# Where VectorE puts three weight splits among the forms of x, at the front of the last two feed-forwards

## The reference, cut to what matters

```
x = layer_norm(ALPHA * x + mix, ln1_g, ln1_b)
u = depthwise_conv_centred(x @ w_up, conv_w, conv_b)        # w_up: 1024 x 5632, 3 taps along the tokens
gate, val = split(u, 2)                                     # 22 tiles of 128 channels each
ffn = (silu(gate) * val) @ w_down                           # w_down: 2816 x 1024
x = layer_norm(ALPHA * x + ffn, ln2_g, ln2_b)
```

## Time and profile before

| | |
|---|---|
| median of 3 runs | 3225.05 us (3224.18 to 3225.34) |
| time of the profiled execution | 3225.85 us |
| span of the profiled execution | 3224.0 us |
| mean granted clock of TensorE | 0.995 |
| busy, share of the span | PE 98%, PEld 81%, DVE 58%, ACT 44%, POOL 42% |
| DMA | 288.40 MB, mean 89 GB/s |

### The profile page before, as it was taken

The page is one execution under the profiler, slowest core; times in us unless marked ns, Lnnn a source line. Parts: engine busy times, 40 slices in busy tenths (PEclk is TensorE's granted clock), DMA queues, the critical chain, the costliest instruction groups (busy, mean ns, idle before and its releaser), DMA issues.

```text
span 3224.0 us, 43797 instructions
## 1 busy us (share of the span) xinstructions
PE 3163.0 (98%) x17576; PEld 2597.2 (81%) x17576; DVE 1862.2 (58%) x2975; ACT 1419.4 (44%) x2559; POOL 1370.2 (42%) x788
## 2 busy tenths in 40 slices
PE   7999999999999999999999999999999999989998
PEld 4876888888875557888886888899997788879997
DVE  5877366323337663423325686388872768468885
ACT  4323422222246774423334545355553544455554
POOL 2221423232254445444552234645555234445555
PEclk9999999999999999999999999999999999999999
DMA  7323334122132002333232120422233121213231
GB/s 270 110 97 119 127 101 153 54 63 69 51 116 103 14 14 92 113 89 110 74 124 79 46 67 20 142 79 98 97 120 112 46 67 49 63 58 107 97 99 67
DMA packets 88246, 288.40 MB, mean 89 GB/s; under 512 B 10059, under 2 KB 12683, under 8 KB 87276
## 3 DMA queue, kind: packets, MB, share of 16 engines
q1 hardware_dynamic: 88044, 285.60, 27.2%
HBM read 283.47 MB, written 2.10 MB: 89 GB/s over the span
## 4 chain that ended last, share of the span: by engine, by line
PE 87%; DVE 3%; issue 3%; POOL 3%; ACT 2%; DMA 1%; SPq 0%; POOLq 0%; DVEq 0%; ACTq 0%
PE ps L611 16%; PE ps L614 15%; PE ps L612 15%; PE ps L3429 4%; PE ps L3428 4%; PE ps L3427 4%; PE ps L670 2%; PE ps L672 2%; PE ps L671 2%; PE ps L2262 2%; PE ps L3114 1%; PE ps L590 1%; PE ps L585 1%; POOL WL L559 1%; PE ps L586 1%
## 5 line engine op out<-in xcount | busy, mean ns | idle before, releaser
L559 POOL TENSOR_TENSOR WL<-ring,WH 128x1024 fp32r<-128x1024 f32 (+4 forms) x461 | 961.6, 2091 | 1340.9 <-ACT WH L549 1340.5
L549 ACT CAST WH<-ring 128x1024 fp32r<-128x1024 f32 (+4 forms) x497 | 448.9, 904 | 507.4 <-PE ps L614 385.8
L611 PE MATMUL ps<-FR,WH 128*128 128x512 f32 x1120 | 419.2, 374 | 0.2
L611 PE MATMUL ps<-HX,WH 128*128 128x512 f32 x1048 | 413.8, 395 | 4.2 <-DVE WL L537 4.2
L614 PE MATMUL ps<-HX,WL 128*128 128x512 f32 x1048 | 411.9, 393 | 0.0
L612 PE MATMUL ps<-HX,WH 128*128 128x512 f32 x1048 | 410.5, 392 | 0.0
L612 PE MATMUL ps<-FR,WH 128*128 128x512 f32 x1120 | 410.0, 373 | 0.0
L614 PE MATMUL ps<-FR,WL 128*128 128x512 f32 x1120 | 389.2, 373 | 0.0
L611 PEld LDWEIGHTS ps<-FR,WH 128*128 128x128 f32 x1120 | 210.4, 188 | 45.6 <-DVE FR L3327 1.1
L612 PEld LDWEIGHTS ps<-FR,WH 128*128 128x128 f32 x1120 | 210.5, 188 | 36.0
L611 PEld LDWEIGHTS ps<-HX,WH 128*128 128x128 f32 x1048 | 197.6, 189 | 48.6 <-DVE WL L537 4.7
(11 more groups left out here) (456 smaller groups left out, 7049.6 us busy)
## 6 DMA issues: line engine op xcount, KB each, us to landing
ring<-in_ffn_w_up SPq DMA_DIRECT2D x88, 512.0 KB, 3.6
ring<-in_w_up SPq DMA_DIRECT2D x88, 512.0 KB, 3.6
ring<-in_w_mod SPq DMA_DIRECT2D x64, 512.0 KB, 3.8
ring<-in_w_in_tok SPq DMA_DIRECT2D x40, 512.0 KB, 3.7
ring<-in_w_mod_columns SPq DMA_DIRECT2D x32, 512.0 KB, 4.3
ring<-in_w_in_feat SPq DMA_DIRECT2D x32, 512.0 KB, 3.5
ring<-in_w_down SPq DMA_DIRECT2D x48, 320.0 KB, 3.9
ring<-in_ffn_w_down SPq DMA_DIRECT2D x32, 384.0 KB, 3.1
```

The lines of the kernel that those rows point to most:

```text
L549: act.copy(WH[:, p % SPLITS, 0:n], src).then_inc(*split.a.up("high", p))
L559: pool.tensor_tensor(WL[:, p % SPLITS, 0:n], unit_source(p)[0], WH[:, p % SPLITS, 0:n], ALU.subtract).then_inc(*low_up(split.g, p))
L611: pe.matmul(o, high, xh, first, False)
```

## The change

The third unit's split goes from POOL to DVE, in layer 1 alone. `forms_v` gets another order in both layers, and the two splits of `between` are taken apart: `between(0)` is that of the fourth unit, `between(1)` that of the fifth.

```
-        in_vector |= {g_.last for t_ in L_ffb for g_ in (*t_.groups[3:5], *t_.groups[-8:])}
+        in_vector |= {g_.last for t_ in L_ffb for g_ in (*t_.groups[3:5], *t_.groups[-8:])}
+        in_vector.add(L_ffb[1].groups[2].last)
...
-            for k in range(4):
+            def form(k):
                 (wait for the kept tile k + 4, and the three instructions of form k)
-            for k in range(4):
-                if k == 2:
-                    between()
-                low(k)
+            form(0)
+            form(1)
+            low(0)
+            between(0)
+            low(1)
+            form(2)
+            form(3)
+            low(2)
+            between(1)
+            low(3)
...
+            if L.groups[2].last in in_vector:
+                rest_v(dve, L.groups[2].last)
             sums_1_2(FRONT)
-            forms_v(dve, qf, lambda: (rest_v(dve, L.groups[3].last), rest_v(dve, L.groups[4].last)))
+            forms_v(dve, qf, lambda x: rest_v(dve, L.groups[3 + x].last))
             sums_1_2(FRONT + 1)
```

## The result

The changed kernel takes 3231.53 us (median of 16 runs, 3229.79 to 3234.39), the kernel before 3226.11 us (16 runs, 3224.18 to 3228.22): 5.4 us more, ratio 1.0017 with the interval 1.0011 to 1.0024. Forecast were 3226.5 us and a range up to 3229.6: it is slower than that. The new waits came as forecast; the clock behind them, and what PE waits further on, did not. The forecast started from 3225.05 us, the median of three runs; with 16 runs the kernel before lies 1.1 us higher. As a difference the range ended at +4.55 us, and +5.4 was measured. It is 0.17%, less than the 0.2% that I had taken for the least that can be told, and with 16 runs of each kernel it is clear of the noise.

A forecast was written before the change was run, and what follows sets the result against it. PE, busy 98% of the span, was taken to bound the kernel, so only its waits count. +2.5 us in layer 0 and -1.1 in layer 1 gave +1.4 on 3225.05, so 3226.5 us; range 3223.8 to 3229.6.

The forecast's parts named there:

- Fourth unit in layer 1: Layer 1: PE's wait for the fourth unit shrinks from 4.25 to 2.0 us, the unit beginning 3.6 us earlier.
- the fifth: Layer 1: PE waits 2.0 us for the fifth unit, beginning it 4.5 us ahead of before.
- the sixth: Layer 1: PE waits about 3.2 us for POOL's split of the sixth unit; 1.1 us of lead are left.
- Layer 0: DVE's later taps delay POOL's split of the sixth unit; PE newly waits 2.3 to 2.7 us, 2.5 taken.
- The low part of 2.22 us: Layer 1: DVE's low part of x, slowed during POOL's split, returns to 0.74 us; PE is 1.3 us earlier.
- the sum of +1.4: Whole kernel: +2.5 us in layer 0 less 1.1 in layer 1; the forecast itself, chance 0.62.
- the price of the clock: Behind the new waits in both layers: a clock fall costs 0 to 2.9 us each; nothing was taken.
- the idle stretch that kept it: 2844 to 2849 us: PE idle 2.0 of 5 us with the clock at 1.00; reason for pricing falls at nothing.
- Behind it PE takes the sixth unit and the seventh and goes on: Layer 1, behind the sixth unit's wait: PE goes on; a gain of 0.7 to 1.5 us is kept.
- That adds 0 to 0.4: Layer 0, tenth unit: DVE's late fourth sum may delay ACT's cast and POOL's split, adding 0 to 0.4 us.
- The fourth rival: The clock falls in both layers, at PE's restart at the sixth unit: +7.2 us, 3232.3 us; chance 0.04.
- The warning that I had cited: Gaps without matmuls halve PE's rate; by it each longer wait would cost 2.9 us, giving the second or fourth rival's time.

The follow-up runs named there:

- e4: The changed kernel with idle matmuls filling PE's new waits (11 in layer 0; 8, 8, 13 in layer 1); +4.3 us against the kernel before (1.0013).
- e6: The changed kernel run once more, unaltered; 3230.46 against 3225.11 us for the kernel before, +5.35 (1.0016).
- e8: The changed kernel with the third unit's split of layer 1 back on POOL; 3232.18 against 3225.11 us for the kernel before, +7.1 (1.0022).
- e2: The kernel before with the new order in layer 0 alone, layer 1 as before; 3228.20 us, +2.6 against the kernel before (1.0011).
- e12: The kernel before run once more for a second profile of its one long wait; 3225.38 against 3225.39 us, 0.0.
- e1: The changed kernel with layer 0's old order back, layer 1 as changed; 3227.55 against 3225.56 us for the kernel before, +2.0 (1.0005).
- e3: The changed kernel with ACT casting the sixth unit early, ahead of the first gate's silu; 3233.28 against 3225.56 us for the kernel before, +7.7 (1.0025).
- e11: e1 with idle matmuls filling layer 1's three waits (8, 8, 13); +1.5 us against the kernel before (1.0002).
- e7: The kernel before with 18 idle matmuls in PE's one long wait, ahead of layer 1's fourth unit; -1.0 us against the kernel before (0.9997).
- e9: e5 with DVE doing the low part of the first tile's result sooner; 3223.14 against 3225.39 us for the kernel before, -2.3 (0.9992).
- e5: The kernel before with layer 1 reordered on DVE and ACT after what the waits need; 3226.37 against 3225.11 us, +1.3 (1.0002).

## Why the prediction was wrong

**The waits were right.** Fourth unit in layer 1: forecast 2.0, measured 1.9; the fifth (seen in e4, where filling keeps the clock: 7.47 us from the fourth to the fifth, less 5.44) 2.0 and 2.0; the sixth 3.2 and 3.0. Layer 0: forecast 2.3 to 2.7, measured 2.5; at full clock the stretch up to the seventh unit costs 2.8 us (e6), against the 2.5 taken. Layer 1 up to the seventh unit without a fall is 41.98 us, 0.86 less than the profile before; forecast 1.1. DVE stood 1.1 us ahead of the fourth unit's split in layer 0, as said. The low part of 2.22 us went, for 1.15 us of gain (e8), against the 1.3 that I took. Up to the seventh unit, then, the sum of +1.4 is measured as +1.9.

**The first step that failed is the price of the clock**: "A fall costs at most the 2.9 us seen, at least nothing; I take nothing, since three of the four are nearer to the idle stretch that kept it". The runs say otherwise. The duration of the unit behind each wait, at full clock 5.6 us with its start:

| wait of PE | kernel: duration of the unit behind it, us |
|---|---|
| 4.25 | before 8.32, e2 7.16, e12 7.10 |
| 3.0 | after 8.28, e1 7.17, e6 7.19, e8 5.57 |
| 2.48 | after 7.16, e8 7.22, e2 5.57, e6 5.57 |
| 1.94 | clock 0.77 in after, e1, e6 and e8, and in e3 behind 1.90 (hidden) |
| filled | e4 5.58 and 5.57, e11 5.58, e7 5.61 |

The clock fell behind half of the waits of 2.5 us, behind three of four of 3.0, and behind all four of 1.94. Three kernels with another order add four waits: it fell behind 1.90 and 2.69 us in e3 and 1.86 in e9, and held behind 2.68 in e3. The falls behind 1.94 cost nothing, because the fifth unit was not ready anyway, as the prediction had it. The sixth's fall has no cover at the unit itself, where it costs 1.6 us, or 2.7 once.

My reason for taking nothing was a row of one profile, and it was chance. The idle stretch that kept the clock there (1.04 us, and 1.69 ahead of the pair) stands ahead of the pair of layer 1 in all 14 profiles, and in 10 of them the granted clock of the 5 us behind it is below 1.00, in e12, the same kernel once more, among them. The 5 us behind it, in the kernel before:

```profile
2849.70:2854.70 5.00, 4.87 (x18) 3.12 (x19) 5.00 (x6) 2.02 (x3) 5.00 (x4) 1.00 0.00 0
```

and in e12, the idle stretch and the 5 us behind it:

```profile
2845.30:2850.30 5.00, 3.03 (x42) 1.75 (x31) 3.50 (x7) 2.56 (x6) 2.41 (x2) 1.00 0.25 100
2851.10:2856.10 5.00, 5.00 (x16) 4.03 (x17) 5.00 (x6) 1.93 (x3) 5.00 (x4) 0.70 0.00 0
```

**The second step that failed is "Behind it PE takes the sixth unit and the seventh and goes on"**, with "That adds 0 to 0.4" in layer 0. 21.8 us behind the start of the seventh unit PE waits for another split of POOL, 0.3 us before the change. With the new order it is 0.90 to 0.97 us where the sixth unit ran at full clock, and 0.2 where the clock fell and PE came later. In e6, layer 0, ACT stands 1.13 us for DVE's taps ahead of the cast for that split (0.46 before), so it is the same late chain (PE, then ACT):

```profile
2141.18 0.38 PE L3434 MATMUL ps<-XH,WH 128*128 128x256 f32 x1 [0.97 <-POOL WL L560]
```

```profile
2137.08 0.60 ACT L3606 ACTIVATE ps<-T 128x512 f32<-128x512 f32 x1 [1.13 <-DVE T L3628]
```

So each layer is longer than the stretch up to the seventh unit tells. From the first matmul of the pair of layer 0 to that of layer 1, and from there to the last matmul of the program:

| sixth unit | layer 0, us | layer 1, us |
|---|---|---|
| as before | before 765.76, e12 765.80 | before 363.51, e12 362.21, e2 362.33 (the fourth fell) |
| new order, full clock | e6 769.20, e2 769.22, e4 769.22 | e4 363.39, e11 363.34 (e8 364.50, with a pair 1.15 longer) |
| new order, clock fell | after 770.04, e8 770.02 | e1 364.19, e6 364.18, after 365.55 |

At full clock the change costs 3.4 us in layer 0, where 2.5 was forecast and 3.1 was the upper end, and in layer 1 it gains 0.1 against the profile that I used, where 1.1 was forecast. A fall of the clock at the sixth unit makes PE late enough to take the later wait away, so 0.8 of its 1.6 us are left; with the long one it is 2.2, of which 0.3 lie in the pair.

**A third error stands in what I compared with.** The one long wait of the kernel before was priced with its worst fall, and the gain of the change was counted against it. Its three profiles from pair to seventh unit are 42.84, 41.66 and 41.57, mean 42.0: 0.8 us less than the one I used.

Together, an estimate from these few profiles: the forecast's +1.4; behind the seventh unit and by small sizes +0.9 in layer 0 and +1.0 in layer 1; the clock, which fell in two of four profiles in layer 0 and in three of four in layer 1, 0.8 / 2 = +0.4 and (2.2 + 0.8 + 0.8) / 4 = +1.0; and the fall that the kernel before does not always have, +0.8. That is +5.5 us, measured +5.4 and +5.35. The fourth rival, a fall in both layers, is what the profile of the changed kernel shows, and I gave it 0.04; its price, 2 x 2.9 us, was too high, for of a fall 0.8 to 2.2 us are left. The prediction's range held the forecast and one fall, not the two, and not what PE waits further on.

The warning that I had cited, from the Trainium skill, "TensorE: Matmul & The Clock Gate", section "Why this matters for your kernels" (a gap without matmuls puts the engine back to half rate), was the better guide than my row, though it speaks of longer gaps than most of these waits. The traces show such falls, and behind shorter gaps too: behind 12 of the 16 waits from 1.86 to 3.01 us, with a granted clock of 0.62 to 0.77 in the stretch that follows.

**Why the order costs at all** is shown by e3, e5 and e9: DVE's order is one serial chain, from the forms to the eighth unit's split. In layer 0 the new order makes DVE stand for ACT three times (3.5 us) where it had stood 0.2 us, with the same work ahead of the taps, and PE had not waited for the fourth unit; so the whole chain behind comes 3.5 us later, where 0.8 us of slack were. In layer 1 it does bring the fourth unit forward, but DVE stands for ACT there too; the 1.5 us that POOL had cost DVE came off, and 1.1 for the third unit's split came on.

## What to carry to other kernels

When one unit's wait goes, follow the engine's whole chain on to the first unit with less slack than the new delay: the gain of 4.1 us at the fifth unit of layer 1 was 0.8 at the sixth. Then look on behind that unit: a wait of 0.2 or 0.3 us there tells that nothing is left for a delay; here it cost 0.7 us in either layer. A new idle stretch of PE of 2 us or more is to be priced with the chance of a fall of the clock, not with none; and whether the clock falls behind an idle stretch, before or after, must be known from more than one profile before anything is counted on it. Units of equal duration in the trace make that easy to read.

## What the runs showed of the hardware

The fall of the clock behind one and the same wait (2.48 us, the same in four profiles to a hundredth) came in two executions and not in two others, with 7.2 against 5.57 us for 24 matmuls. Behind an idle stretch in two pieces (1.04 and 1.69 us, the same in 14 profiles) it came in 10 of 14. Matmuls that do no work, put in the wait, kept the clock at 1.00 in all eight places tried (four in e4, three in e11, one in e7). A DVE sum of two tiles in SBUF, 0.69 us by itself, took 2.71 us beside a POOL split of 2.97 us (e3), and ended 0.55 us after that split: it looks as if the one stood until the other was done.
